# New order at both ends of the scan and in the last stage, and sixteen sums moved to GpSimd, in a two-layer RWKV-7 and attention decoder

## The reference

```
def wkv7_step(state, inp):                     # one token; the prompt runs over 1024 of them
    r_t, w_t, k_t, v_t, a_t, b_t = inp
    sa = einsum('bhij,bhj->bhi', state, a_t)
    state = state * w_t[:, :, None, :] + sa[..., None] * b_t[:, :, None, :] + v_t[..., None] * k_t[:, :, None, :]
    y = einsum('bhij,bhj->bhi', state, r_t)
    return state, y

# after the scan, in rwkv7_time_mix
    y = (y - mu) * rsqrt(var + LNX_EPS) * lnx_g + lnx_b       # over each head
    bonus = sum(r * k * r_k) * v
    out = ((y + bonus) * g) @ w_o

# around it, in reference
    xp = xp + mp[2] * op
    xp = xp + mp[5] * square(relu(hp @ w_up)) @ w_down        # hp: the normed xp
```

## Time and profile before

| | us |
|---|---|
| median of 3 runs | 2743.39 |
| lowest and highest | 2740.34, 2746.11 |
| profiled execution | 2751.72 |
| its span | 2749.7 |
| PE busy | 2586.4 (94%) |
| DVE busy | 1458.8 (53%) |
| ACT busy | 1123.9 (41%) |
| POOL busy | 895.8 (33%) |
| mean granted clock of PE | 0.973 |

### The profile page before, as it was taken

How to read it: one execution, slowest core, us unless ns; L and a number is a source line. 1 busy time by engine, 2 the same in 40 slices (tenths; PEclk the granted TensorE clock), 3 DMA queues, 4 the chain that set the end, 5 groups by cost and what they waited for, 6 DMA issues and landing times. The chain is left out here.

```text
span 2749.7 us, 52825 instructions
## 1 busy us (share of the span) xinstructions
PE 2586.4 (94%) x21466; PEld 2433.3 (88%) x21466; DVE 1458.8 (53%) x2782; ACT 1123.9 (41%) x2250; POOL 895.8 (33%) x725
## 2 busy tenths in 40 slices
PE   4989999989889999999999999998988999999998
PEld 2769898878789999999999998887988999999997
DVE  6358777246677211212212354875686666565665
ACT  5447633325455312202202343665465443434334
POOL 1122212147721221122211302112168874445442
PEclk7999999999989999999999999998999999999998
DMA  8878768788781322222222312212222321111112
GB/s 335 327 261 259 233 238 250 218 192 199 193 262 47 106 79 70 92 92 76 88 91 77 105 57 64 72 46 78 66 62 85 93 89 51 47 51 51 51 47 78
DMA packets 383096, 342.29 MB, mean 124 GB/s; under 512 B 115526, under 2 KB 352522, under 8 KB 375916
## 3 DMA queue, kind: packets, MB, share of 16 engines
q1 hardware_dynamic: 351788, 298.20, 35.5%
q10 hardware_dynamic: 25408, 21.41, 2.7%
q0 software_dynamic: 5664, 19.33, 1.9%
HBM read 258.75 MB, written 78.78 MB: 123 GB/s over the span
## 5 line engine op out<-in xcount | busy, mean ns | idle before, releaser
L1405 PE MATMUL t_acc<-t_area,wH 128*128 128x258 f32 (+1 forms) x1552 | 465.4, 300 | 16.0 <-DVE shared L1823 5.3
L1406 PE MATMUL t_acc<-t_area,wH 128*128 128x258 f32 (+1 forms) x1552 | 460.1, 296 | 0.0
L1407 PE MATMUL t_acc<-t_area,wL 128*128 128x258 f32 (+1 forms) x1552 | 459.9, 296 | 0.0
L556 POOL TENSOR_TENSOR wL<-raw,wH 128x1024 fp32r<-128x1024 f32 x61 | 146.2, 2398 | 666.9 <-ACT wH L681 666.9
L1405 PEld LDWEIGHTS t_acc<-t_area,wH 128*128 128x128 f32 x1552 | 295.7, 191 | 22.7 <-issue 12.1
L1406 PEld LDWEIGHTS t_acc<-t_area,wH 128*128 128x128 f32 x1552 | 295.7, 191 | 0.2
L1407 PEld LDWEIGHTS t_acc<-t_area,wL 128*128 128x128 f32 x1552 | 295.3, 190 | 0.1
L1698 DVE SCALAR_TENSOR_TENSOR X<-t_acc,mod,X 128x258 f32<-128x258 f32 (+4 forms) x456 | 237.5, 532 | 105.6 <-PE t_acc L1407 74.8
L1360 POOL TENSOR_TENSOR wL<-raw,wH 128x512 fp32r<-128x512 f32 x126 | 168.4, 1343 | 258.1 <-ACT wH L1536 257.0
L577 PE MATMUL t_acc<-twoH,wH 128*128 128x344 f32 x744 | 239.8, 322 | 2.6 <-DVE twoL L902 1.6
L579 PE MATMUL t_acc<-twoH,wL 128*128 128x344 f32 x744 | 237.5, 319 | 0.0
(11 more groups left out here) (561 smaller groups left out, 6684.7 us busy)
## 6 DMA issues: line engine op xcount, KB each, us to landing
ada_ring<-in_ada_w SPq DMA_DIRECT2D x24, 1024.0 KB, 9.3
shared<-in_ada_w SPq DMA_DIRECT2D x24, 1024.0 KB, 6.3
raw<-in_mlp_up SPq DMA_DIRECT2D x84, 256.0 KB, 2.9
t_plain<-in_mlp_down SPq DMA_DIRECT2D x84, 256.0 KB
raw<-in_mlp_down SPq DMA_DIRECT2D x32, 512.0 KB, 4.2
raw<-in_mlp_up SPq DMA_DIRECT2D x30, 512.0 KB, 4.1
kvrb_hx<-hx_saved ACTq DMA_DIRECT2D x16, 516.5 KB, 4.7
kvr_work<-scr_L SPq DMA_DIRECT2D x16, 516.0 KB, 5.8
```

The costliest lines, as they stand in the source:

```text
L556: pool.tensor_tensor(low, raw_of(w), high.bitcast(F32), ALU.subtract).then_inc(s_low, 1)
L1405: pe.matmul(out, high, h, start=begin, stop=False, skip_group_check=True)
L1406: pe.matmul(out, high, l, start=False, stop=False, skip_group_check=True)
L1407: return pe.matmul(out, low, h, start=False, stop=end, skip_group_check=True)
```

## The change

It has three parts.

At the start of the scan, ACT writes `scr_Smp` and SP reads it back, in place of POOL; POOL's order in a chunk is scaled, centred, values, removed, read, faded (`removed` is cut in three, its operations are the same); DVE's `products` and `outputs` stand behind the update of S and no longer in front of the sum into pD.

At the end of the scan, work of the next stage is put in: ACT's `affine` of pieces 0 and 1 in the last chunk but one, DVE's `adds` of them and ACT's `rounded` (the high) in the last, and high and low of panels 0 and 1 between the lagging turns; it leaves `stage_tail`. For that the places of these results are allocated earlier (`o_place`, `HHnext`). DVE's norm of the step's output is cut in two (`centre`, `spread_of`) and comes later, POOL's last step operations are put between `scaled` and `centred`, PE's turn of the step's output (`by_channel`) and ACT's copy of it (`kept`) come last. In the tail PE runs the high parts of pieces 0 and 1 on panels 0 and 1 first.

In the last stage `load_x` is cut in halves; `token_sum` is POOL's, ahead of its weights of round 0; highs and lows of the token sums in round 0 stand elsewhere; and POOL makes the low of P2 ahead of the two weight sums in every round but the first.

The diff, cut to its core:

```diff
+                for k in range(2):
+                    for m in range(2):
+                        high, low = place("o", m)
+                        pe.wait_ge(s_ph, k + 1)
+                        pe.wait_ge(s_lowD, m + 1)
+                        pe.matmul(acc[m][:, 0:TT], high[:, k, :], HH[:, k, third[0]], start=(k == 0), stop=False)
+                        pe.matmul(acc[m][:, 0:TT], low[:, k, :], HH[:, k, third[0]], start=False, stop=False)
+                    for m in range(2):
+                        pe.wait_ge(s_pl, k + 1)
+                        pe.matmul(acc[m][:, 0:TT], place("o", m)[0][:, k, :], HL[:, k, third[0]], start=False, stop=False)
+                for k, m in [(0, 2), (1, 2), (2, 0), (2, 1), (2, 2)] + [(k, 3) for k in range(3)] + [(k, m) for k in range(3, DB) for m in range(4)]:
...
-            affine(0)
-            high(0)
-            affine(1)
-            prepared(0)
-            high(1)
             high(2)
-            prepared(1)
             affine(2)
...
-            adds(0)
+                dve.sem_inc(s_ph, 2)
+                dve.sem_inc(s_lowD, 2)
+                dve.sem_inc(s_high, 2)
+                dve.sem_inc(s_paff, 2)
+                dve.sem_inc(s_padd, 4)
+            prep_low(0)
+            prep_low(1)
             dve.wait_ge(net.s_lateY, 32)
-            own_low(0)
-            prep_low(0)
-            adds(1)
-            own_low(1)
-            prep_low(1)
             own_low(2)
             adds(2)
             own_low(3)
...
-    SUMS = {(2, 3): (0, 2), (2, 4): (2, 4), (2, 5): (4, 7), (2, 6): (7, 10), (2, 7): (10, 12), (3, 0): (12, 16)}
     LOWS = {(3, m): (2 * m - 2, 2 * m) for m in range(1, DB)}
-    LOWS_FIRST = {"P1": (14, 20), "P2": (20, 24), "P6": (24, 28)}
+    HIGHS_FIRST = {"P1": (14, 16), "P2": (20, 24), "P6": (24, 28)}
+    HIGHS_THEN = {"P1": (16, 20)}
+    LOWS_FIRST = {"P1": (14, 16), "P2": (16, 24), "P5": (24, 28)}
...
             def load_x(q):
-                sp.wait_ge(s_pl, (q + 1) * DB)
-                sp.dma_start(X[:, :, quarter[q]], net.x_saved[:, :, quarter[q]]).then_inc(s_x[q], 16)
+                for h in range(2):
+                    b = slice(4 * h, 4 * h + 4)
+                    sp.wait_ge(s_pl, q * DB + 4 * h + 4)
+                    sp.dma_start(X[:, b, quarter[q]], net.x_saved[:, b, quarter[q]]).then_inc(s_x[q][h], 16)
...
+            for n in range(16):
+                token_sum(n)
             q11, q12, q21, q22, extra = (raw_unit(n) for n in range(5))
             for r, (_, _, mid) in enumerate(rounds):
+                if r == 1:
+                    pool.wait_ge(s_cl, 28)
                 low(weight_at["p", r, "P1"])
+                if r:
+                    low(weight_at["p", r, "P2"])
...
-                low(weight_at["p", r, "P2"])
+                if r == 0:
+                    low(weight_at["p", r, "P2"])
...
+    def vectors(self, sp):
+        sp.wait_ge(self.s_rows, 16)
         for i in range(5):
-            pool.dma_start(self.vec[:, i, :], self.net.sSmp[i].rearrange("s (h d) -> (s h) d", d=HD)).then_inc(self.s_vec, 16)
+            sp.dma_start(self.vec[:, i, :], self.net.sSmp[i].rearrange("s (h d) -> (s h) d", d=HD)).then_inc(self.s_vec, 16)
...
+                elif s == 1:
+                    smp.vectors(sp)
...
             def work(c, k, i, last):
                 scaled(c, k)
+                centred(c, k)
                 pool.wait_ge(smp.s_S, i * 16 + 16)
-                pool.wait_ge(smp.s_value, 16)
-                pool.wait_ge(smp.s_vec, 80)
+                pool.wait_ge(smp.s_vec, 96)
                 smp.values(pool, c)
-                centred(c, k)
-                smp.removed(pool, c)
+                if not last:
+                    smp.removed(pool, c)
+                    smp.read(pool, c)
+                    smp.faded(pool, c)
...
-            smp.vectors(pool)
             for c in range(NCH):
                 work(c, c % BODY, c // BODY, c == NCH - 1)
-            for k in range(Y_LAG):
+            scaled(NCH, 0)
+            smp.removed(pool, NCH - 1)
+            centred(NCH, 0)
+            smp.read(pool, NCH - 1)
+            for k in range(1, Y_LAG):
                 scaled(NCH + k, k)
-                if k == 0:
-                    centred(NCH, 0)
+            smp.faded(pool, NCH - 1)
...
-                    smp.by_channel(pe, quarters(pU)[:, 0, :])
+            smp.by_channel(pe, quarters(pU)[:, 0, :])
...
+                if left == 1:
+                    for q in range(2):
+                        affine(q)
+                if left == 0:
+                    for q in range(2):
+                        rounded(q)
...
+            own_high(0)
...
+                if k == 0:
+                    own_high(1)
+            smp.kept(act, quarters(pU)[:, 0, :])
+            act.wait_ge(s_oph, 2)
+            act.wait_ge(s_ohigh, 2)
...
-                smp.outputs(dve, c)
                 mean(c, k, c)
-                smp.products(dve, c)
+                if not left:
+                    for q in range(2):
+                        adds(q)
                 dve.wait_ge(s_D, c + 1)
                 dve.tensor_tensor(pD[:], pD[:], S[:], ALU.add).then_inc(s_sum, 1)
-                if not last:
+                if left:
                     masked(c + 1, 1 - g, 1)
                 dve.wait_ge(s_sum, c + 1)
                 for half in range(2):
                     b = slice(4 * half, 4 * half + 4)
                     dve.tensor_tensor(S[:, b], pD[:, b], net.pend[:, b, bass.ds(c, 1)].to_broadcast([128, 4, HD]), ALU.mult).then_inc(s_S, 1)
+                if left:
+                    smp.products(dve, c)
+                    smp.outputs(dve, c)
...
+            inverse(NCH)
+            smp.products(dve, NCH - 1)
+            mean(NCH, 0, NCH)
+            dve.wait_ge(s_yi, NCH + 1)
+            variance(NCH)
+            smp.outputs(dve, NCH - 1)
+            own_low(0)
+            inverse(NCH + 1)
+            dve.wait_ge(s_yi, NCH + 2)
+            variance(NCH + 1)
+            smp.outputs(dve, NCH)
+            smp.centre(dve)
+            inverse(NCH + 2)
+            smp.spread_of(dve)
+            smp.scaled(dve)
+            own_low(1)
```

166 lines of the change are left out of this document (98 added, 68 removed).

## The result

The changed kernel took 2766.25 us (median of 7 runs, 2756.16 to 2774.38) against 2749.92 us of the kernel before (7 runs in the same comparison). The ratio is 1.0056 with a 95% interval of 1.0039 to 1.0073: slower by some 15 us. The forecast was 2746.5, +3.1 us, with a range from 2732 to 2756. It was wrong. Part of the miss is the base: the forecast stood on 2743.4, the median of three runs of the kernel before, and the median of seven is 6.5 us higher. The measured ratio on the forecast's own base would be some 2759, still outside the range.

The account below looks back on a forecast made before the run. TensorE, busy 94% of the span, was taken as the bound, so edits count only at its gaps. -6.2 + 4.5 - 1.0 - 5.8 + 11.6 = +3.1 us on 2743.4 gave 2746.5 us, range 2732 to 2756.

Parts of the forecast that it names:

- Half rounds: Last stage, rounds 2 to 9: sums behind low(P2) delay low(d0) and PE's hidden units, +11.6 us; bounds 0 and +20.
- The price of a round: Half rounds: PE would begin hidden at 2175.9 instead of 2174.11, +1.75 us a round, 14 us over eight.
- The absorption: Half rounds: rounds whose raw weights already come late by DMA absorb part of the price, estimated at 2.4 us.
- The rival with its full price: Half rounds: sums cost 2.55 us in each of eight rounds, 20.4 instead of 11.6; time 2755.3; chance 0.18.
- Projection: Last stage: sixteen sums fit POOL's idle time at no cost; X in halves removes DVE waits PE hardly sees, 0.
- Round 0: Last stage: spread lows and highs and DVE freed of sums start PE's hidden units sooner, -5.8 us; bounds -3 and -10.
- Scan start: Scan's first chunk: products no longer hold up the sum into pD, -6.2 us; gain bounds 3.6 and 8.2.
- The bound of 8.2: Scan start: largest gain, 8.2 us, if the step's vectors arrive at 590.5.
- 3.5 us in chunk 1: Scan start: excess left because vectors arrive at 592.5 while chunk 1's DVE work is due at 589.0.
- The rival with vectors in time: Scan start: a transfer's small fixed cost lets the vectors arrive in time, 3.5 us more gain, 2743.0; chance 0.08.
- Scan end: Scan's hand-over to the tail: SP waits for the sample's later store, +4.5 us; bounds +1 and +6.5.
- Tail start: Tail: PE's first matmul no longer waits 5.95 us, but later pieces keep it waiting longer, -1 us; bounds 0 and -4.

Follow-up runs that it names:

- experiment 1: Changed kernel with POOL's order in the rounds as before (both weight sums ahead of the low of P2); ratio 0.9972 to the kernel before.
- experiment 2: Kernel before with only the low of P2 put ahead of the two weight sums from round 1 on; ratio 1.0050.
- experiment 12: Kernel before with X loaded in halves and nothing else; ratio 0.9986.
- experiment 11: Kernel before with only the sixteen token sums moved to POOL, X loaded in whole quarters; ratio 1.0007.
- experiment 3: Kernel before with the changed last stage (token sums on POOL, X in halves, new highs and lows), POOL's order of the rounds as before; ratio 0.9981.
- experiment 9: Kernel before with only DVE's products and outputs put behind the update of S in every chunk; ratio 0.9985.
- experiment 13: Kernel before with the last stage of experiment 3 and DVE's order of experiment 9 in all chunks but the last; ratio 0.9962 to the kernel before.
- experiment 14: Experiment 13 with the step's vectors written by ACT and read by SP, and POOL's centred ahead of values; ratio 0.9945 to the kernel before.
- experiment 4: Changed kernel with the last stage as before, so only the scan's two ends and the tail's start are new; ratio 0.9985 to the kernel before.
- experiment 7: Experiment 1 with the step's last POOL operations ahead of the three scaled, so the sample's store leaves earlier; ratio 0.9965 to the kernel before.
- experiment 8: Experiment 7 with POOL's loads of panels 4 and 5 held back until the highs of pieces 2 and 3; ratio 0.9958 to the kernel before.

## Why the prediction was wrong, by its steps

**Half rounds, the step that failed.** The mechanism was the one that came about, down to the place and the engine: without the two sums ahead of low(d0) the loss is gone (experiment 1), and with them alone it is there (experiment 2). Its size was forecast as +11.6 and measured as +20.9 (+18.5 in experiment 2, and 19.3 between the changed kernel and experiment 1). Three terms make the 9.3 us between.

The price of a round was put at 1.75. From P2's start on PE to hidden's start it now takes 4.0 to 4.1 us, where it took 1.9 to 2.7, and the eight rounds together give +16.1 in place of 14. Sums of 1.25 and a low of 1.3 us had been assumed; in the changed order these three took 1.47, 1.23 and 1.44 (half of 2.88).

The absorption, 2.4 us, was taken from no row, and there was none in these stretches. The raw weights that come late in rounds 3 to 5 come late in front of P2, and what the sums add comes behind P2: those rounds pay as much as the others, but for one that had 2.74 us before.

The remaining 4.8 us were not in the sum at all. Over D4, PE is busy 6.6 us longer with the same matmuls, at a clock of 0.94 and not 0.99; some 2 us of smaller waits are gone in return. Here are D4 before and D4 changed:

```profile
2027.67:2220.07 192.40, 180.66 (x1442) 175.81 (x1441) 126.99 (x273) 98.82 (x204) 164.73 (x120) 0.99 0.29 87
```

```profile
2022.93:2236.25 213.32, 187.25 (x1440) 183.55 (x1441) 142.84 (x275) 101.93 (x207) 169.56 (x121) 0.94 0.27 80
```

In the changed kernel the clock falls to the lower of its two levels six times in this stretch. Five times it falls within 1 us behind a hidden start and its wait of 2.4 us, once behind a wait for the low of P2 (3.56 us, at 2103.36); behind the other hidden starts it stays. These are 5 us each behind the starts at 2160.67 and 2186.01, with 44 matmuls in one and 32 in the other:

```profile
2161.00:2166.00 5.00, 5.00 (x44) 5.00 (x43) 4.02 (x11) 1.76 (x4) 2.92 (x3) 1.00 0.35 105
2187.00:2192.00 5.00, 5.00 (x32) 5.00 (x32) 2.95 (x9) 1.99 (x4) 2.92 (x3) 0.68 0.34 105
```

Experiment 2 has the same waits at a clock of 0.98, and there the part outside of these stretches is 2.3 us. That the waits bring the clock down fits these rows; no run tests it by itself, and some of it is within D4's scatter.

The rival with its full price (20.4, chance 0.18) comes near in its number, but not by its reason: it had 2.55 us a round with nothing given back, and the rounds cost 2.0. That its total fits is luck.

**Projection, "0" for the halves of X.** Wrong, by 6 us of D3 in the good direction (experiment 12). I looked for PE's waits in the projection and stopped there. DVE's four waits for X, 22.8 us, were mostly hidden from PE in the projection; what they cost came out after it, in round 0, where all that PE waits for from DVE came 5.6 us later than it had to.

**Round 0, -5.8.** The number was right (-5.5), and that is luck in part. The spread of highs and lows and the sums, which I had named as causes, do take away PE's wait for DVE. But the sums move hidden's start by nothing without the halves of X (experiment 11), and both together by 1 us at most with them (experiments 3 and 12). What would be late next, POOL in round 1, was forecast rightly.

**Scan start, -6.2.** Measured -6.9 for DVE's order (experiment 9) and another 1 to 5 for the loads' move and the order of POOL that went with it (152.5 against 150.2 to 151.7, and experiments 13 and 14). The bound of 8.2 was too low. What I priced as remaining, 3.5 us in chunk 1, turned out as two longer chunks of +0.5 and +1.1. The term that was off is the landing of the loads: 5.2 us behind the last issue, as on POOL's queue before, against 1.4 in the changed kernel and 2.6 in experiment 4. The rival with vectors in time, chance 0.08, came true for the most part. Its sum was off as well: with the forecast's own last issue at 587.7, a landing of 2 us gives 589.7 and not "before 589". And 9.6 less 3.5 is 6.1, not 6.2; nothing hangs on that.

**Scan end, +4.5.** Right in its mechanism; measured +6.0 (experiments 1 and 4). Half of it is the store; behind it stand the lagging turns, which with the store early still end 2.6 us later after the last copy of U than before (experiment 7: 19.8 against 17.3 us). That part was missing from the sum. In the trace it is there before the first of the turns starts on POOL: DVE's four early additions took 0.51, 0.93, 1.04 and 1.24 us in the changed kernel, 3.7 in all where 2.1 plus 0.5 had been counted, and POOL's operations beside them 1.31 in place of 1.04; behind them, in experiment 7, a product of the step took 1.58 in place of 0.72. How the 2.6 us divide among these wasn't tried.

**Tail start, -1.** Wrong in sign: +1.6. That POOL's panel loads would move to the stage's start stood in the order of the program and was not priced; holding two of them back took 3.4 us off this stretch (experiment 8).

**The sum.** By the distances the change is -9.1 + 6.0 + 1.6 - 5.5 + 20.9 = +14, which lies within the interval of the timed ratio (+11 to +20). The scan's two ends and the tail's start together are worth -1.5, the last stage without its order of sums -6.

## What to carry to other kernels

An operation that fills a wait has no price where it stands and can have nearly its full price elsewhere (here 2.0 us a round for two sums of 2.7): before moving it behind the wait, ask what stands in the new place, and charge its duration there, less the slack that the rows show, for each turn of the loop, with nothing taken off for absorption unless a row shows an event that doesn't move along. An engine's idle time that hides from the bottleneck in one stage can surface in the next; follow the late engine forward, not only the bottleneck's waits backward. When a change has many parts, swap the parts between the two kernels: here one edit made the loss, two made nearly all the gain, and the part that it was named for made nothing that could be measured.

## What the runs showed of the hardware

Between two profiles, unchanged code in one stretch took some 5 us more or less, and what the view shows changed beside it is PE's clock. From the start of PE's last transposes of attention weights (1887.05 before, 1892.87 changed) to the last stage's first matmul (1901.98 and 1902.72) it took 14.9 us and 9.9. These are the 18 us up to 1902 in both: the clock (the figure behind POOL's) is 0.64 in one and 0.93 in the other, with 100 and 136 matmuls.

```profile
1884.00:1902.00 18.00, 14.52 (x100) 13.10 (x100) 6.13 (x14) 6.82 (x19) 0.00 (x0) 0.64 0.00 1
```

```profile
1884.00:1902.00 18.00, 14.28 (x136) 11.79 (x134) 11.20 (x22) 10.49 (x29) 0.00 (x0) 0.93 0.01 1
```

The first weight sum, the same 128x512 operation, took 1.30 us on POOL in the earlier trace rows and 1.52 in the changed order, where DVE's t_area<-shared,t_area (0.43 us at 2181.74) ran beside its start. That the one comes from the other wasn't tried.

POOL's first product started 1.4 us after the last of five loads of 32 KB was issued from SP, and 1.9 to 3.2 us in experiments 4, 7 and 14; with the loads issued by POOL itself it was 5.2, and 4.8 and 5.6 in experiments 9 and 13. POOL's write of 160 KB in front of them was waited for 5.15, 5.34 and 6.20 us (before, experiments 9 and 13).
